# Query, key and latent-query tiles of a two-layer decoder kernel, reshaped for TensorE's column groups and shared between VectorE and ScalarE

## The reference

```python
hc, gc, gb, cq, ckv, kpe = _split_last(a @ w_in, (512, 512, 512, 384, 256, 32))
...
ckv = _rms(ckv, kv_norm)
kpe = _rope(kpe, cos, sin)
q = (_rms(cq, q_norm) @ w_uq).reshape(b, t, 8, 64 + 32)
q_nope = q[..., :64]
q_pe = _rope(q[..., 64:], cos, sin)        # x1*c - x2*s, x2*c + x1*s on the two halves of 16
q_lat = jnp.einsum('bthn,rhn->bthr', q_nope, w_uk)
o_lat = attend(q_lat, q_pe, ckv, kpe)
```

## Time and profile before

| | |
|---|---|
| median of 3 runs | 1524.11 us (1523.51 to 1524.64) |
| the profiled execution | 1524.06 us |
| its span, first to last instruction | 1522.3 us |
| TensorE busy | 1479.8 us, 97% |
| VectorE busy | 1019.9 us, 67% |
| ScalarE busy | 266.3 us, 17% |
| mean granted TensorE clock | 0.986 |
| the stretch of the change | about 50 to 110 us |

### The profile page before, as it was taken

One profiled execution on the slowest core, in us unless ns is written; L12 is line 12 of the kernel. 1 busy time (PEld: TensorE's weight loads), 2 busy tenths in 40 slices (PEclk: granted clock), 3 DMA queues, 4 the chain that ended last, 5 costly groups with the idle time before them and its releaser, 6 DMA issues.

```text
span 1522.3 us, 18973 instructions
## 1 busy us (share of the span) xinstructions
PE 1479.8 (97%) x7084; PEld 1188.6 (78%) x7084; DVE 1019.9 (67%) x2073; ACT 266.3 (17%) x564; POOL 103.0 (7%) x114
## 2 busy tenths in 40 slices
PE   7999999799999999999999999999999999999996
PEld 6866676488888888888877778788888888888875
DVE  3663444677876766766856786887866767767845
ACT  4012122222101001011233321121001011011223
POOL 0222333000000000000200001300000000000100
PEclk9999999899999999999999999999999999999998
DMA  7546776321222222222203211222222222222201
GB/s 277 160 120 208 223 233 212 114 80 69 78 82 82 82 83 83 84 83 98 84 28 143 84 56 56 87 83 83 83 80 78 79 79 79 81 83 97 84 28 59
DMA packets 40557, 154.59 MB, mean 102 GB/s; under 512 B 6737, under 2 KB 19442, under 8 KB 27794
## 3 DMA queue, kind: packets, MB, share of 16 engines
q1 hardware_dynamic: 35346, 136.60, 25.8%
q0 software_dynamic: 5120, 16.78, 3.6%
HBM read 150.33 MB, written 3.02 MB: 101 GB/s over the span
## 4 chain that ended last, share of the span: by engine, by line
PE 93%; DVE 5%; issue 1%; DMA 0%; ACT 0%; DVEq 0%; SPq 0%
PE psum L595 69%; PE psum L565 8%; PE psum L701 6%; PE psum L745 1%; PE psum L859 1%; PE psum L795 1%; PE psum L550 1%; PE psum L891 1%; PE psum L810 1%; PE psum L659 0%; PE psum L821 0%; PE psum L868 0%; PE psum L942 0%; PE psum L730 0%; DMA ring<-in_weights 0%
## 5 line engine op out<-in xcount | busy, mean ns | idle before, releaser
L595 PE MATMUL psum<-arena 128*128 128x272 f32 x2016 | 480.4, 394 | 0.0
L595 PEld LDWEIGHTS psum<-arena 128*128 128x128 f32 x2016 | 383.9, 191 | 79.3 <-DVEq L1253 0.2
L1257 DVE TENSOR_TENSOR arena<-psum,arena 128x272 f32<-128x272 f32 x564 | 248.8, 441 | 243.4 <-PE psum L595 220.2
L595 PE MATMUL psum<-B,ring 128*128 128x272 f32 x736 | 186.2, 395 | 2.6 <-ACT B L988 2.0
L595 PE MATMUL psum<-arena,ring 128*128 128x272 f32 x672 | 167.7, 392 | 0.0
L595 PEld LDWEIGHTS psum<-B,ring 128*128 128x128 f32 x736 | 139.7, 191 | 32.6 <-ACT B L988 2.4
L595 PE MATMUL psum<-A,ring 128*128 128x272 f32 x608 | 152.6, 393 | 1.6 <-DVE A L1736 1.5
L595 PEld LDWEIGHTS psum<-arena,ring 128*128 128x128 f32 x672 | 127.4, 190 | 26.0
L595 PEld LDWEIGHTS psum<-A,ring 128*128 128x128 f32 x608 | 115.4, 190 | 26.1 <-DVE A L1736 1.9
L1011 ACT ACTIVATE arena<-psum 128x272 f32<-128x272 f32 x84 | 33.3, 396 | 547.4 <-PE psum L595 547.3
L595 PE MATMUL psum<-B,arena 128*128 128x272 f32 x368 | 92.9, 394 | 0.0
(11 more groups left out here) (238 smaller groups left out, 1388.3 us busy)
## 6 DMA issues: line engine op xcount, KB each, us to landing
ring<-in_weights SPq DMA_DIRECT2D x98, 1024.0 KB, 4.8
arena<-in_keys SPq DMA_DIRECT2D x128, 144.0 KB, 2.7
h<-in_xT SPq DMA_DIRECT2D x8, 544.0 KB, 8.7
arena<-in_attw SPq DMA_DIRECT2D x1, 3072.0 KB, 18.5
out_yT<-A SPq DMA_DIRECT2D x8, 272.0 KB, 2.3
arena<-in_pemb SPq DMA_DIRECT2D x2, 544.0 KB, 6.4
ring<-in_weights SPq DMA_DIRECT2D x2, 512.0 KB, 6.7
arena<-in_bias SPq DMA_DIRECT2D x1, 640.0 KB, 8.3
```

What stands on the lines that cost most here:

```text
L595: end = pe.matmul(bank(g, n), lhs[:, c, :], x(c), start=c == 0, stop=c == 3)
L1257: ins = dve.tensor_tensor(out, bank(g, n), more, ALU.add)
```

## The change

- **Rotary key tile.** `in_ab(5)` becomes its own loop: only the 64 columns that aren't zeros are weights, and the two token halves go to rows 0 to 63 and 64 to 127 of one bank. VectorE scales each half into `kx[0:64]`.
- **Queries.** The swapped columns are no longer in the weights. A rotary tile is copied to SBUF by ScalarE (`rotary_copy`), and a 128x128 permutation `perm` as weights gives the swapped tile. The tiles come in the order heads 0, rotary 0, heads 1, swapped 0, rotary 1, heads 2, swapped 1, heads 3.
- **Latent queries.** `qs` becomes the weights (64 x 32) and `wukT` the moving operand (256 columns), eight products in four column groups of bank 4; ScalarE copies the result, six transposes turn it, and VectorE copies it to `qx` as before, from banks 4 and 5.
- **ScalarE** takes the odd heads of `Q` and `K`.
- **Order.** The latent products come between key tiles 1 and 2, the transposes between key tiles 2 and 3, the value tiles before the score pairs; `turn(0)`, `new_max`, `block_max(0)`, `new_exp`, `block_exp(0)` and `turned(0)` move into the first steps of the loop, and score pair 2 from its step 0 to step 1.
- **Transfers.** The attention weights come in two DMAs. The rotary key's store, GpSimd's gather of slot 0 and ScalarE's copies of it wait for `kpe_ready`, given after two key tiles.

```diff
-            sp.dma_start(arena[:, 4352:10496], a["attw"]).then_inc(attw_loaded, 16)
+            sp.dma_start(arena[:, 4352:6784], a["wuq"]).then_inc(attw_loaded, 16)
+            sp.dma_start(arena[:, 7424:10496], a["attw"]).then_inc(attw_loaded, 16)
...
-            in_ab(5)
+            t, w = T_COL[5], ring[:, ring_of(2), :].rearrange("p (k m) -> p k m", k=KD)
+            free(t)
+            for k in range(KD):
+                for i in range(2):
+                    last = pe.matmul(slot(t)[64 * i:64 * i + 64, 0, 0:TH], w[:, k, P:P + 64], A[:, k, TH * i:TH * i + TH],
+                                     start=k == 0, stop=k == KD - 1)
+            last.then_inc(psum_full, 1)
...
-            for m in range(8):
-                tile(T_UQ + m, lambda k: wuq[:, k, m * P:(m + 1) * P], cq, 3)
+            def heads(c):
+                tile(T_HEADS[c], lambda k: wuq[:, k, c * P:(c + 1) * P], cq, 3)
+            def rotary(c):
+                tile(T_ROT[c], lambda k: wuq[:, k, (4 + c) * P:(5 + c) * P], cq, 3)
+            def swapped(c):
+                pe.wait_ge(rot_copied, c + 1)
+                tile(T_SWAP[c], lambda k: perm, rot(c), 1)
...
+            keys_up(0)
+            keys_up(1)
             pe.wait_ge(qs_ready, 1)
+            pe.wait_ge(psum_free, T_N0 + 1)
             for hd in range(H):
+                rows, j = slice(64 * (hd % 2), 64 * (hd % 2) + 64), hd % 4
+                last = pe.matmul(psum[32 * j:32 * j + 32, 4, R * (hd // 4):R * (hd // 4) + R], qs[rows, hd // 2, :],
+                                 wukT[rows, hd // 2, :], start=True, stop=True)
+            last.then_inc(ql_full, 1)
+            keys_up(2)
+            pe.wait_ge(ql_copied, 1)
+            for e in range(2):
                 for c in range(3):
                     n = 96 if c < 2 else 64
-                    pe.matmul(qlat[0:n, hd % 2, c, hd // 2 * 32:hd // 2 * 32 + 32], wukT[rows, hd // 2, 96 * c:96 * c + n],
-                              qs[rows, hd // 2, :], start=True, stop=True)
+                    pe.transpose(ql_bank(e, c)[0:n], qlt[:, e, 96 * c:96 * c + n], ident[:])
             for c in range(2):
-                last = pe.transpose(qlat[0:32, c, 3, :], ckv[:, c, TP:T], ident[:])
-            last.then_inc(psum_full, 1)
+                last = pe.transpose(psum[0:32, 4, 2 * P + P * c:3 * P + P * c], ckv[:, c, TP:T], ident[:])
+            last.then_inc(ql_turned, 1)
+            keys_up(3)
...
+            def heads_odd(c):
+                act.wait_ge(heads_scaled, c + 1)
+                act.activation(halves(Q[0:64, 2 * c + 1, :]), pv(T_HEADS[c])[64:128], ACT.Copy, scale=SCALE).then_inc(q_odd, 1)
+            def rotary_copy(c):
+                act.wait_ge(psum_full, T_ROT[c] + 1)
+                act.activation(halves(rot_at[c]), pv(T_ROT[c]), ACT.Copy).then_inc(rot_copied, 1)
+            def keys_odd(c):
+                act.wait_ge(psum_full, T_UK + c + 1)
+                act.activation(K[0:64, 2 * c + 1, :], slot(T_UK + c)[64:128, 0, :], ACT.Copy).then_inc(k_odd, 1)
...
+            heads_odd(0)
+            rotary_copy(0)
+            heads_odd(1)
+            rotary_copy(1)
+            heads_odd(2)
+            heads_odd(3)
+            keys_odd(0)
+            keys_odd(1)
+            act.wait_ge(ql_full, 1)
+            act.activation(qlt, psum[:, 4, :].rearrange("p (e r) -> p e r", e=2), ACT.Copy).then_inc(ql_copied, 1)
+            keys_odd(2)
+            keys_odd(3)
+            act.wait_ge(kpe_ready, 1)
...
+            def heads(c):
+                t = T_HEADS[c]
+                full(t)
+                link(dve.tensor_scalar(qs[:, c, :], slot(t)[:, 1, TH - TS:TH], SCALE, None, ALU.mult))
+                dve.nop().then_inc(heads_scaled, 1)
+                link(dve.tensor_scalar(halves(Q[0:64, 2 * c, :]), pv(t)[0:64], SCALE, None, ALU.mult))
+                dve.wait_ge(q_odd, c + 1)
                 dve.nop().then_inc(psum_free, 1)
+            def rotary(c):
+                dve.wait_ge(rot_copied, c + 1)
+                link(dve.scalar_tensor_tensor(halves(rbuf[:, 0, :]), pv(T_ROT[c]), SCALE, halves(rope[:, 4, :]),
+                                              ALU.mult, ALU.mult))
+                dve.nop().then_inc(psum_free, 1)
```

More of the change, by code:

```diff
@@ new lines, in _, with keys_up @@
+            heads(0)
+            rotary(0)
+            heads(1)
+            swapped(0)
+            rotary(1)
+            heads(2)
+            swapped(1)
+            heads(3)
+            def keys_up(m):
+                t = T_UK + m
+                free(t)
+                for k in range(2):
+                    last = pe.matmul(slot(t)[:, 0, :], wuk[:, k, m * P:(m + 1) * P], ckv[:, k, 0:TP],
+                                     start=k == 0, stop=k == 1)
+                last.then_inc(psum_full, 1)
@@ L804, in turn_out @@
                 last.then_inc(ot_full, 1)
[L806 to L816, removed]
             for i in range(4):
@@ L823, in _ @@
                 last.then_inc(psum_full, 1)
-            turn(0)
+            pe.wait_ge(ql_ready, 1)
+            score_pair(0)
+            score_pair(1)
+            score_new()
             def paged(n):
@@ L836, in paged @@
                     turn_out(1)
-                if step < 2 and k + 1 < N_BLOCKS:
+                if step < 2 and 0 < n and k + 1 < N_BLOCKS:
                     score_pair(2 * (k + 1) + step)
@@ L1572, in paged @@
                 k, step = divmod(n, 4)
-                if step == 0 and k < N_BLOCKS:
+                if n == 0:
+                    new_max()
+                    block_max(0)
+                elif n == 1:
+                    new_turned()
+                    turned(0)
+                elif step == 0 and k < N_BLOCKS:
                     turned(k)
@@ L1609, in _ @@
             scaled(4, ckv[:, 1, :])
-            scaled(5, kx)
+            full(T_COL[5])
+            for i, half in enumerate((N1, N2)):
+                rows = slice(64 * i, 64 * i + 64)
+                link(dve.tensor_tensor(kx[0:64, half], slot(T_COL[5])[rows, 0, 0:TH], rstd[rows, half], ALU.mult))
+            dve.nop().then_inc(psum_free, 1)
             norm_root(2, T_NKV, sq[:, 1, :], R)
@@ L1615, in _, with swapped, keys_even @@
             dve.wait_ge(c_loaded, 64)
[L1617 to L1621, removed]
-                dve.nop().then_inc(psum_free, 1)
+            def heads(c):
[5 more added lines that the diff above has]
+                dve.wait_ge(q_odd, c + 1)
+                dve.nop().then_inc(psum_free, 1)
+            def rotary(c):
+                dve.wait_ge(rot_copied, c + 1)
+                link(dve.scalar_tensor_tensor(halves(rbuf[:, 0, :]), pv(T_ROT[c]), SCALE, halves(rope[:, 4, :]),
+                                              ALU.mult, ALU.mult))
+                dve.nop().then_inc(psum_free, 1)
+            def swapped(c):
+                full(T_SWAP[c])
+                link(dve.scalar_tensor_tensor(halves(rbuf[:, 1, :]), pv(T_SWAP[c]), SCALE, halves(rope[:, 5, :]),
+                                              ALU.mult, ALU.mult))
+                dve.nop().then_inc(psum_free, 1)
+                for j in range(4):
+                    link(dve.tensor_tensor(Q[64:96, 4 * c + j, :], rbuf[32 * j:32 * j + 32, 0, :],
+                                           rbuf[32 * j:32 * j + 32, 1, :], ALU.add))
+            def keys_even(c):
+                full(T_UK + c)
+                link(dve.tensor_copy(K[0:64, 2 * c, :], slot(T_UK + c)[0:64, 0, :]))
+                dve.wait_ge(k_odd, c + 1)
+                dve.nop().then_inc(psum_free, 1)
+            heads(0)
+            rotary(0)
+            heads(1)
+            swapped(0)
+            rotary(1)
+            heads(2)
+            swapped(1)
+            heads(3)
+            dve.nop().then_inc(qs_ready, 1)
+            keys_even(0)
+            keys_even(1)
             link(dve.tensor_tensor(rbuf[64:96, 0, :], kx[0:32, :], rope[0:32, 4, :], ALU.mult))
@@ L1625, in _ @@
             link(dve.tensor_tensor(ssum[64:96, :], rbuf[64:96, 0, :], rbuf[64:96, 1, :], ALU.add))
[L1626 to L1637, removed]
-            re = lambda x: x.rearrange("p (b h t) -> p b h t", b=NB, h=H)
[L1639 to L1644, removed]
+            dve.nop().then_inc(kpe_ready, 1)
+            keys_even(2)
+            dve.wait_ge(ql_turned, 1)
+            re = lambda x: x.rearrange("p (b h t) -> p b h t", b=NB, h=H)
+            for e in range(2):
+                for c in range(3):
+                    n, i = (96 if c < 2 else 64), 3 * e + c
+                    at = psum[0:n, 5, P * i:P * i + P] if i < 4 else psum[0:n, 4, P * (i - 4):P * (i - 4) + P]
+                    link(dve.tensor_copy(re(qx[0:n, c, :])[:, :, 4 * e:4 * e + 4, :],
+                                         at.rearrange("p (h b t) -> p b h t", h=4, b=NB)))
             link(dve.tensor_copy(re(qx[64:96, 2, :]), Q[64:96, :, TP:T].rearrange("p h (b t) -> p b h t", b=NB)))
```

(4 more changed lines are left out.)

59 lines of the change are left out of this document (33 added, 26 removed).

## The result

| | before | changed | ratio |
|---|---|---|---|
| first measurement, median | 1524.38 us | 1508.18 us (1504.55 to 1511.34, 4 runs) | 0.9885 [0.9868, 0.9902] |
| second measurement, median | 1524.77 us | 1510.4 us (1509.36 to 1511.34, 4 runs) | 0.9902 [0.9887, 0.9918] |
| profiled execution, first | 1524.06 us | 1511.34 us | |
| its span | 1522.3 us | 1509.5 us | |

By its medians the changed kernel is 16.2 and 14.4 us faster; the sum had 14.35. The first ratio makes 1506.9 us of the 1524.38 (0.9885 x 1524.38), 1.1 under the low end of my range (1508.0 to 1513.4); the second makes 1509.8, the forecast. Both are medians of four executions of one kernel, so that the second hits to 0.1 us is luck as much as the first's miss is chance. The changed stretch has to be judged apart from what differs from one execution to the next.

What follows compares the result with a forecast made beforehand. TensorE, busy in 97% of the span, was taken as the bound. Savings of 3.4 + 4.1 + 4.55 + 2.16 + 0.15 = 14.35 us from 1524.1 gave 1509.8 us; range for 8 in 10: 1508.0 to 1513.4.

Steps and rivals of the forecast that it cites:

- rotary key tile with the norm sum: Before the loop: tile with 64 weight columns and overlapping halves takes 3.9 us, 3.4 saved; norm sum 1.85 us.
- query tiles, wait in them: Eight query tiles, 80 records instead of 96: 18.65 instead of 22.72 us, 4.1 saved, with a stall of 0.3.
- latent products, transposes: Latent queries: eight products 1.07 us, eight transposes 1.05, in sum 2.1 instead of 6.67, 4.55 saved.
- four key tiles: Key tiles, same work at full clock: 6.96 instead of 9.12 us, 2.16 saved if the clock stays up.
- stretch saved: From latent column 4's start to the attention loop's first record: the loop begins 15.0 us earlier, at 94.5 us.
- of it back in the loop: The first turn, four transposes of 0.60 us together, moves into the attention loop; from its start to the end 0.6 longer.
- rival 3: Rotary key tile: its halves don't overlap at 272 columns, 3.4 us lost, 1513.2 us; chance 3%.
- rivals 1 and 5: 1: clock falls once near latent queries, 1513.2 us, 14%. 5: clock half from 50 us through queries, 1555 us, 3%.
- rival 4: What is saved before the loop is lost inside it by transfers: nothing gained, 1524 us; chance 2%.
- Rival 2: VectorE and ScalarE hold TensorE up, reading one bank in turn or by late first steps: 2.5 us, 1512.3; 9%.
- The range's term for the clock elsewhere: At the loop's end: a half-level clock stretch shifted against the waits there may cost 1.5 us more or less.
- my case: The forecast with no rival coming true: 1509.8 us, own range 1508.2 to 1511.5; chance 69%.

Runs made afterwards that it cites:

- filled forms: The changed kernel with products without use in front of TensorE's waits: at two waits 1510.06 us, at eight 1504.83 us.
- experiment 14: The kernel before with products without use before eight waits, third further profile: 1523.24 us, stretch 65.5 us.
- experiment 10: The changed kernel itself, unaltered, one more profiled execution: 1505.75 us, stretch 52.2 us.
- experiment 8: The changed kernel with products without use before eight TensorE waits: 1504.83 us, ratio to the kernel before 0.987.
- experiments 8 and 9: Products without use before eight waits, in the changed kernel (1504.83 us) and in the kernel before (1523.32 us; its group at the higher clock, median 1520.2).
- experiment 11: The changed kernel itself, unaltered, another profiled execution: 1510.69 us, stretch 52.2 us.

## Why the prediction was right, and where it wasn't

| step | forecast | measured |
|---|---|---|
| rotary key tile with the norm sum | 3.9 + 1.85 | 3.82 + 2.04 |
| query tiles, wait in them | 18.65, 0.3 | 18.85, 0.3 |
| latent products, transposes | 1.07 + 1.05 | 1.00 + 0.88 |
| four key tiles | 6.96 | 7.06 |
| value tiles, scores | 6.96 + 4.19 | 7.08 + 4.19 |
| stretch saved | 15.0 | 14.7 |
| of it back in the loop | 0.6 | 0.1 |

**The parts.** Each piece of the stretch was right to 0.2 us; for the queries the direct sum, 22.72 less 3.66 and 0.2 of waits, would have given the 18.86 measured. The column groups overlap at 272 columns as L891 did at 128 (rival 3 falls): the tile's 32 records take 3.82, 0.119 each. Behind the 64-column tile the norm sum took 0.19 us more, and behind the latent products a key tile 0.19 more (1.91 against 1.72 for the others). The Trainium skill (TensorEngine Tiling, Key Properties) names a drain of TensorE at a change of tiling mode; these two agree with it, and its price here is small. The clock stayed at 1.00 from 42 us to the loop in all six profiles of the changed kernel and its filled forms: rivals 1 and 5 fall, and with the time saved rival 4. By the Trainium skill (TensorE: Matmul & The Clock Gate, Part 4) the eight transposes could have pulled the clock down; here they didn't. Of the turn's 0.6 us in the loop little shows: it is there with 0.49, but the pieces around it take as much less: the loop's first three steps are 17.7 us before and 17.6 after.

**VectorE and ScalarE.** Rival 2 didn't come. Two readers on two row halves of a bank cost nothing: ScalarE's copies took 0.62 against the 0.70 that I took, VectorE's 0.72 as in the kernel before. But I undervalued what the sharing is for. Put back, it costs 4.7 us, not 2.4: VectorE has no gap over 0.24 us from 64 to 95 us there, and a third of the 14.7 rests on its being relieved. In the changed kernel itself my schedule was short as well: I had VectorE's first value copy 1.0 us ahead of TensorE's want of that slot; it ended at 89.36 and the fourth value tile began at 89.42. That nothing waited longer there was luck.

**The clock in the sum.** I counted 2.16 us for the key tiles as won back from the clock, and part of the latent queries' 4.55: in experiment 14, with the clock full until 90 us, these take 5.44 + 0.32 instead of 6.13 + 0.54. But in the kernel before VectorE would have held the last key tile even at a full clock. Half the fall was 1.5 us of the stretch and the rest could bring some 0.2, so 1.5 to 1.7 of the 14.7 (an estimate beyond the 1.5) are what the clock alone would have given back. The other 13 are TensorE's shorter work together with VectorE's relief: the parts were right, but they don't add up singly.

**What failed.** The range's term for the clock elsewhere: I wrote that within my case "a half-level stretch shifted against those waits may cost 1.5 us more or less", and put the case's own range at 1508.2 to 1511.5. Ten executions of the changed kernel lie from 1504.55 to 1511.34, and the three fastest (1504.55, 1505.75, 1506.65) are under it. The profiles show why: the stretch is 52.2 us in every one, while the clock falls at other places, 170 to 1400 us later, in number and length as it comes. Between the first profile and experiment 10 these falls make 5.2 us of the 5.5 by which the spans differ, where my term had 1.5; with the places filled (experiment 8) the spread is 1.0. In the sum I had put this term at nothing, as if both kernels lost alike. The mechanism of the stretch was right; it is this term's size that was wrong. I had read only the place at 280 us, and not those at 843 and 925 and the last, which the trace of before held as well. With four executions the median moves with them, and the ratio of the first measurement went 1.1 us under my range. The kernel before moves too: its times go from 1520.89 to 1526.81 in these measurements. The profiled execution that I compared first was the slowest of its four.

**Outside the stretch** the two first profiles differ by -12.8 + 14.7 = 1.9 us: 0.8 by a later start of the latent columns, 0.1 in the loop, 1.2 at its end, where both lose 6.8 us of clock but the kernel before pays 1.5 for it and the changed one 2.8, 0.7 at the final norm, and 0.8 less between (rounded). But for the turn that moved into the loop I had none of these.

**The difference of the steady kernels.** The stretches with the clock up should differ by about 13, not by the 15.4 of experiments 8 and 9. The profiles of experiments 14 and 8 differ by 18.4: 13.3 in the stretch, 1.8 by a later start of the latent columns, 1.4 by a wait near 813 us (2.6 instead of 1.2), and 1.9 by a fall of the clock right behind it. Of the 1.8, 1.2 is TensorE's wait for its first weights at the start of the program (8.8 against 7.6). The wait near 813 us is for VectorE, which had itself waited for weights:

```profile
798.89 8.48 DMA ring<-in_weights
```

This transfer takes 8.3 to 8.5 us in the four profiles of the kernel before with the products, and 6.9 to 7.2 in the other twelve. So some 3 us of the 18.4 are arrivals of weights outside the change. How much of them stands in the 15.4, and why that transfer is longer in these four, is open.

## What to carry to other kernels

Where TensorE is the bound, narrow products are worth turning round: weights of 32 columns in four column groups with a wide moving operand did in 1.9 us, transposes included, what took 6.7 (5.8 with the clock nearly full), and the clock stayed up. Price such a form by a row of the same shape in the same trace; it held to 0.2 us. Before giving a range, list every place of the trace where the granted clock is at half, not only those near the change: each may be there or not in the next execution, and may cost what it loses or nothing, so that a change well made can be measured several us off for that alone. And schedule the slower engines with the gaps between their operations: over 53 of these they were 3.3 us.

## What the runs showed that I had not expected

- Useless products before eight waits made the changed kernel steady and faster: 1504.83 us and a spread of 1 us in four executions, against 1510 and 7 in ten. At two places alone they gained nothing in the time. The kernel before gained 1.8 us by its medians and stayed unsteady (1519.28 to 1526.15). The changed kernel with them is the fastest here.
- Most half-level places lose 1.7 or 3.4 us; one in the kernel before lost 5.1 (277.2 to 287.4), and the last one lasts to the end of the program. Two profiles of one kernel had all four at the same times, while other executions had others.
- In the kernel before the mean clock hardly showed in the time: executions with clock 0.986 and 0.990 took 1524.8 and 1524.9. A fall that lies under a wait costs nothing, and the mean doesn't tell where the falls lie.
- A wait of 1.8 us for "issue", with no engine as its cause, stands at one place early in the second layer wherever the clock was up in front of it, in either kernel. Where the clock had fallen just before, it is shorter: 1.3 us behind a fall that lost 1.7 (experiment 11), 0.16 in the kernel before behind one that lost 3.4 (843 to 851 us). So such a fall costs less than it loses. What is waited for there the profile doesn't show.
